# Block products of a ConvFFN: order of VectorE's work around the four pairs, and the rows of decayed sums in one buffer

## What is computed

```python
def conv_ffn(h, P, i):
    g = dwconv(h @ P['ffn_w_gate'][i], P['ffn_conv_w'][i])
    u = h @ P['ffn_w_up'][i]
    return (jax.nn.gelu(g) * u) @ P['ffn_w_down'][i]        # D_FF = 2816

# ssd_scan (layer 0), for each chunk of 128 tokens, direction and head
a_cs = jnp.cumsum(jnp.moveaxis(chunks(dt * a), -1, 1), axis=-1)
seg = a_cs[..., :, None] - a_cs[..., None, :]
decay = jnp.where(causal, jnp.exp(jnp.where(causal, seg, 0.0)), 0.0)
cb = jnp.einsum('bclhn,bcshn->bhcls', cm, bm) * decay
```

## Time and profile before

| | us |
|---|---|
| median of 3 runs | 1918.06 |
| lowest, highest | 1913.84, 1918.71 |
| the profiled execution | 1917.92 |
| its span | 1916.2 |

### The profile page before, as it was taken

How to read it: one execution, slowest core, us unless ns; L and a number is a source line. 1 busy time by engine, 2 the same in 40 slices (tenths; PEclk the granted TensorE clock), 3 DMA queues, 4 the chain that set the end, 5 groups by cost and what they waited for, 6 DMA issues and landing times.

```text
span 1916.2 us, 34733 instructions
## 1 busy us (share of the span) xinstructions
PE 1857.5 (97%) x13240; PEld 1775.7 (93%) x13240; DVE 1182.6 (62%) x2247; ACT 681.0 (36%) x1108; POOL 694.6 (36%) x389
## 2 busy tenths in 40 slices
PE   5999999999999999999999999999999999999997
PEld 3998888888999999999999999977899999999997
DVE  5767788776623777675554354567567676755543
ACT  4443332223313333333333321157433333333332
POOL 1232222223232336355335433433223363453352
PEclk9999999999999999999999999999999999999998
DMA  8335454554533212213212432211322232132221
GB/s 296 108 104 164 143 170 144 167 166 154 174 121 88 77 61 84 74 58 99 76 53 73 145 92 86 89 36 33 103 66 67 59 94 75 58 88 77 60 66 72
DMA packets 263965, 192.76 MB, mean 101 GB/s; under 512 B 25514, under 2 KB 247078, under 8 KB 263350
## 3 DMA queue, kind: packets, MB, share of 16 engines
q1 hardware_dynamic: 258694, 182.78, 31.2%
q10 hardware_dynamic: 5168, 8.58, 1.3%
HBM read 181.29 MB, written 10.04 MB: 100 GB/s over the span
## 4 chain that ended last, share of the span: by engine, by line
PE 86%; issue 5%; DVE 4%; ACT 2%; POOL 1%; DMA 1%; SPq 0%; POOLq 0%; ACTq 0%; DVEq 0%
PE ps L712 46%; PE ps L715 23%; PE ps L1044 5%; PE ps L782 2%; POOL w_lo L629 1%; PE ps L1190 1%; PE ps L974 1%; PE ps L1170 1%; PE ps L1136 1%; DVE x L2192 1%; DVE act_lo L1827 1%; DVE w_mix L2178 1%; ACT sp L1619 1%; PE ps L1209 0%; PE ps L959 0%
## 5 line engine op out<-in xcount | busy, mean ns | idle before, releaser
L629 POOL TENSOR_TENSOR w_lo<-raw,w_hi 128x1024 fp32r<-128x1024 f32 x212 | 532.0, 2513 | 1031.5 <-ACT w_hi L1243 1025.3
L712 PE MATMUL ps<-act_hi,w_hi 128*128 128x322 f32 x2752 | 640.5, 314 | 4.8 <-DVE act_lo L1827 2.2
L712 PE MATMUL ps<-act_lo,w_hi 128*128 128x322 f32 x2752 | 634.4, 312 | 0.0
L715 PE MATMUL ps<-act_hi,w_lo 128*128 128x322 f32 x2752 | 633.1, 311 | 0.0
L712 PEld LDWEIGHTS ps<-act_hi,w_hi 128*128 128x128 f32 x2752 | 462.4, 190 | 18.2 <-issue 14.9
L712 PEld LDWEIGHTS ps<-act_lo,w_hi 128*128 128x128 f32 x2752 | 464.2, 189 | 3.4 <-issue 3.4
L715 PEld LDWEIGHTS ps<-act_hi,w_lo 128*128 128x128 f32 x2752 | 467.0, 190 | 0.0
L1243 ACT ACTIVATE w_hi<-raw 128x1024 fp32r<-128x1024 f32 x212 | 222.7, 1052 | 250.1 <-PE ps L715 191.8
L1044 PE MATMUL ps<-quad_hi,w_hi 128*128 128x322 f32 x336 | 106.7, 318 | 8.4 <-DVE x L2192 8.4
L1911 DVE SCALAR_TENSOR_TENSOR ft<-fg,par,ft 128x642 f32<-128x642 f32 x44 | 110.6, 2514 | 3.5 <-DVE ft L1910 2.5
L2244 DVE TENSOR_TENSOR fg<-ps,spread 128x642 f32<-128x642 f32 x44 | 36.3, 826 | 115.1 <-PE ps L715 103.9
(11 more groups left out here) (326 smaller groups left out, 2533.3 us busy)
## 6 DMA issues: line engine op xcount, KB each, us to landing
ada<-in_ada_w SPq DMA_DIRECT2D x40, 1024.0 KB, 6.0
raw<-in_ssd_w_in SPq DMA_DIRECT2D x44, 512.0 KB, 3.9
raw<-in_ffn_w_gate SPq DMA_DIRECT2D x44, 512.0 KB, 3.8
raw<-in_ffn_w_up SPq DMA_DIRECT2D x44, 512.0 KB, 3.8
raw<-in_na_w_qkv SPq DMA_DIRECT2D x24, 512.0 KB, 3.7
raw<-in_ffn_w_down SPq DMA_DIRECT2D x32, 320.0 KB, 3.1
first<-in_ada_w SPq DMA_DIRECT2D x16, 512.0 KB, 11.1
raw<-in_mix_w_out SPq DMA_DIRECT2D x16, 512.0 KB, 4.1
```

What stands on the lines that cost most here:

```text
L629: g.tensor_tensor(w_lo[:, s], raw[:, s % RAW], w_hi[:, s], ALU.subtract).then_inc(S["low_split"], 1)
L712: t.matmul(half_out(2 * tset, h), hi, chunk_of(src, k0 + k, cols), start=start and src is src_hi, stop=False)
L715: mm = t.matmul(half_out(2 * tset, h), lo, chunk_of(src_hi, k0 + k, cols), start=False, stop=stop)
```

## The change

In the FFN, `product` is cut in two, `gate_part` and `up_part`. At the end of a part VectorE now does `gate_part(late, 0)`, the four weight sums of the second pair, the four `pair_added`, and only then `up_part(late, 0)` with what follows it. `pair_added` of the first pair makes no weight sums. A11 is no longer added to `x` by itself: `first_sbuf` is added to A12 in PSUM (one `tensor_tensor` of 322 columns) and the sum to `x`. `pair_taken` counts six for each pair, and ScalarE may overwrite `first_sbuf` only when the previous pair's A12 was taken. In the mixer, `sum_rows` is one buffer of 5 x 128 columns, the fifth block being the context chunk's sums; `rows_of` is one matmul of 512 columns, and the context rows are four fp32r matmuls of 128 columns.

```diff
-        sum_rows = [at("sum_rows0", N0 + 2 * ROW, [P, 2 * P], F32R),
-                    nc.alloc_sbuf_tensor_at("sum_rows1", [P, 2 * P], F32R, offset=tri_at + 2 * P * 4)]
+        sum_rows = mix("sum_rows", [P, NC * P], F32R)
...
-            for n in range(LC):
-                bank, off = 4 + 3 * (n // 2), P + n % 2 * P
+            for n in range(NC):
+                bank, off = (4 + 3 * (n // 2), P + n % 2 * P) if n < LC else (4, 3 * P)
                 t.transpose(ps[0:2 * HEADS, bank, off:off + P], sc[:, n, K_SUM, :], ident[:])
...
-                for b in range(2):
-                    mm = t.matmul(ps[:, 5, 2 * b * P:2 * b * P + 2 * P], lhs, sum_rows[b][:], start=True, stop=True)
-                mm.then_inc(S["rows_ready"], 1)
+                t.matmul(ps[:, 5, :], lhs, sum_rows[:, 0:LC * P], start=True, stop=True).then_inc(S["rows_ready"], 1)
...
-                        lhs = col[:, LC * KINDS + K_DA, r, h:h + 1].broadcast_to([P, P])
-                        mm = t.matmul(ps[:, 5, (2 * h + r) * P:(2 * h + r + 1) * P], lhs, tri[:, r, :], start=True, stop=True)
+                        lhs = pick[:, r, h:h + 1].broadcast_to([P, P])
+                        mm = t.matmul(ps[:, 5, (2 * h + r) * P:(2 * h + r + 1) * P], lhs, sum_rows[:, LC * P:NC * P], start=True, stop=True)
...
-                                          (A12, 2, 2), (S4, 3, 2), (A22, 6, 3)):
+                                          (A12, 2, 1), (S4, 3, 1), (A22, 6, 2)):
...
-                            act.wait_ge(S["pair_taken"], TAKEN0 + 7 * (pair - 1) + 2)
+                            act.wait_ge(S["pair_taken"], TAKEN0 + 6 * (pair - 1) + 4)
...
-                    for b in range(2):
-                        row = ps[0:2 * HEADS, 4 + 3 * b, P:3 * P]
-                        st.did(v.memset(sum_rows[b][:].bitcast(F32)[4 * HEADS:P, :], 0.0))
...
+                    st.did(v.memset(sum_rows[:].bitcast(F32)[4 * HEADS:P, :], 0.0))
+                    for bank, c0, c1, off in ((4, 0, 2 * P, P), (7, 2 * P, 4 * P, P), (4, 4 * P, 5 * P, 3 * P)):
...
-                more = q < PAIRS - 1
+                more = 0 < q < PAIRS - 1
...
+                used_product(S2)
                 dve.wait_ge(S["pair_copied"], pair + 1)
-                to_x(A11, 0, 0).then_inc(S["pair_taken"], 1)
-                used_product(S2)
                 tt(both_sbuf[:], ps[:, banks[S2], 0:SW], first_sbuf[:], ALU.add).then_inc(S["pair_taken"], 1)
...
                 used_product(A12)
+                summed = ps[:, banks[A12], 0:SW]
+                st.then_wait(tt(summed, summed, first_sbuf[:], ALU.add))
                 to_x(A12, 0, 0).then_inc(S["pair_taken"], 1)
...
-                    if i % SK == SK - 1:
-                        part, late = i // SK, i + 1
-                        ins = product(late, 0)
+                    if ends:
+                        late = i + 1
+                        gate_part(late, 0)
+                        for j in range(4):
+                            weight_sum(p0 + 1, j)
+                        for q in range(PAIRS):
+                            pair_added(lay, p0 + q, q)
+                        ins = up_part(late, 0)
                         if part < SPARTS - 1:
                             quad_sums(late, 0, ins)
+                            quad_lows(late, 0)
                         else:
                             ins.then_inc(S["ffn_up"], 1)
-                        for q in range(PAIRS):
-                            pair_added(lay, (lay * SPARTS + part) * PAIRS + q, q)
-                        (quad_lows if part < SPARTS - 1 else plain_low)(late, 0)
+                            plain_low(late, 0)
```

More of the change, by code:

```diff
@@ L255, in trunk @@
         sto = mix("sto", [P, 2, NS])
[L258 to L259 removed]
+        sum_rows = mix("sum_rows", [P, NC * P], F32R)
+        assert o[0] <= N0
         wdt = at("wdt", CT + 10240, [P, C, 32])
@@ L1034, in pair_down @@
                 for r, operand, taken in ((A11, 0, before[0]), (S2, 5, before[1]), (S1, 1, before[2]), (S3, 4, before[3]),
-                                          (A12, 2, 2), (S4, 3, 2), (A22, 6, 3)):
+                                          (A12, 2, 1), (S4, 3, 1), (A22, 6, 2)):
                     bank = banks[r]
                     pe.wait_ge(S["pair_low"], 7 * pair + r + 1)
-                    pe.wait_ge(S["pair_taken"], 7 * pair + taken + TAKEN0)
+                    pe.wait_ge(S["pair_taken"], 6 * pair + taken + TAKEN0)
                     if q == 0 and r == A11:
@@ L1981, in _ @@
                     group_taken(0)
-                    for b in range(2):
-                        row = ps[0:2 * HEADS, 4 + 3 * b, P:3 * P]
-                        st.did(v.memset(sum_rows[b][:].bitcast(F32)[4 * HEADS:P, :], 0.0))
-                        st.then_wait(v.tensor_copy(sum_rows[b][0:2 * HEADS, :], row))
-                        st.did(tt(sum_rows[b][2 * HEADS:4 * HEADS, :], row, sum_rows[b][0:2 * HEADS, :], ALU.subtract))
+                    st.did(v.memset(sum_rows[:].bitcast(F32)[4 * HEADS:P, :], 0.0))
+                    for bank, c0, c1, off in ((4, 0, 2 * P, P), (7, 2 * P, 4 * P, P), (4, 4 * P, 5 * P, 3 * P)):
+                        row = ps[0:2 * HEADS, bank, off:off + c1 - c0]
+                        st.then_wait(v.tensor_copy(sum_rows[0:2 * HEADS, c0:c1], row))
+                        st.did(tt(sum_rows[2 * HEADS:4 * HEADS, c0:c1], row, sum_rows[0:2 * HEADS, c0:c1], ALU.subtract))
                 for s in range(4):
@@ L2198, in taken @@
                 def taken(n):
-                    dve.wait_ge(S["pair_taken"], TAKEN0 + 7 * pair + n)
+                    dve.wait_ge(S["pair_taken"], TAKEN0 + 6 * pair + n)
+                used_product(S2)
                 dve.wait_ge(S["pair_copied"], pair + 1)
-                to_x(A11, 0, 0).then_inc(S["pair_taken"], 1)
-                used_product(S2)
                 tt(both_sbuf[:], ps[:, banks[S2], 0:SW], first_sbuf[:], ALU.add).then_inc(S["pair_taken"], 1)
@@ L2206, in pair_added @@
                     weight_sum(pair + 1, 0)
-                taken(2)
+                taken(1)
                 st.did(to_x(S2, 0, 1, sbuf=both_sbuf))
@@ L2228, in pair_added @@
                 used_product(A22)
-                taken(4)
+                taken(3)
                 to_x(A22, 1, 0).then_inc(S["pair_taken"], 1)
@@ L2238, in ffn, with gate_part @@
                 dve.wait_ge(S["rinv_ready"], (3, 5)[lay])
-                def product(i, k):
+                def gate_part(i, k):
                     n = f + k + 1 + 2 * i
@@ L2250, in product, with up_part @@
                     conv(par, w, w + 2 * FC, T, fg[k], ft[k]).then_inc(S["ffn_conv"], 1)
-                    if k == 1 and isinstance(i, int) and i < F_PLAIN // 2 and i % SK == SK - 1:
-                        for j in range(4):
-                            weight_sum((lay * SPARTS + i // SK) * PAIRS, j)
+                def up_part(i, k):
+                    n = f + k + 1 + 2 * i
                     used(b, i, 2 * k + 1)
@@ L2260, in product @@
                     return ins
+                def product(i, k):
+                    gate_part(i, k)
+                    return up_part(i, k)
                 def plain_low(i, k):
@@ L2287, in ffn @@
                 for i in range(F_PLAIN // 2):
+                    part, ends = i // SK, i % SK == SK - 1
+                    p0 = (lay * SPARTS + part) * PAIRS
                     for k in range(2):
                         if k > 0 or i == 0 or i % SK != 0:
-                            quad_sums(i, k, product(i, k))
-                            quad_lows(i, k)
-                    if i % SK == SK - 1:
-                        part, late = i // SK, i + 1
-                        ins = product(late, 0)
+                            gate_part(i, k)
+                            if ends and k == 1:
+                                for j in range(4):
+                                    weight_sum(p0, j)
+                            quad_sums(i, k, up_part(i, k))
+                            quad_lows(i, k)
+                    if ends:
+                        late = i + 1
+                        gate_part(late, 0)
+                        for j in range(4):
+                            weight_sum(p0 + 1, j)
+                        for q in range(PAIRS):
+                            pair_added(lay, p0 + q, q)
+                        ins = up_part(late, 0)
                         if part < SPARTS - 1:
                             quad_sums(late, 0, ins)
+                            quad_lows(late, 0)
                         else:
                             ins.then_inc(S["ffn_up"], 1)
-                        for q in range(PAIRS):
-                            pair_added(lay, (lay * SPARTS + part) * PAIRS + q, q)
-                        (quad_lows if part < SPARTS - 1 else plain_low)(late, 0)
+                            plain_low(late, 0)
                 i = F_PLAIN // 2
```

## The result

| | before | after |
|---|---|---|
| median us (4 runs each) | 1918.38 (1913.84 to 1918.71) | 1906.88 (1905.16 to 1907.59) |
| span of the profiled execution | 1916.2 | 1905.9 |
| TensorE idle in the block products, as traced | 8.4 | 5.6 |

The ratio is 0.9945, 95% interval 0.9933 to 0.9958: by the ratio 10.6 us less (8.1 to 12.9), faster by more than the 0.3% that can be told from no change; the medians are 11.5 apart. The forecast was 1906.8.

What follows compares the result with a forecast made beforehand. TensorE, 97% busy, bounds the kernel, so only removed instructions or its standstills count. Stalls -3.2, clock -4.6, mixer rows -3.6 and a transpose +0.2 sum to -11.2: 1906.8 us, range 1900 to 1915 for 8 in 10.

Steps and rivals of the forecast that it cites:

- Stalls: TensorE's four waits at the third pair's A11: 1.45 us lost in each group, 5.8 in place of 9.0, -3.2 us.
- The chain: VectorE's work in the second pair from both_sbuf to S4's add: 7.9 us, where TensorE comes after 6.47.
- The block of the fourth sum: Second pair: fourth weight sum collides with GpSimd's low part, ending at 744.09, not 743.62; without that 0.95 lost each.
- Clock: TensorE's 1.2 GHz stretches behind three of the four stalls: 2.4 GHz expected kept in all four, -4.6 us.
- Mixer: Context rows as short fp32r matmuls at weight-load price, 0.45 us less in eight steps, -3.6; one more transpose, +0.2.
- The late up work: up_part of the late tile after the fourth pair: costs nothing, covered with 1.9 us to spare before the next gate tile.
- VectorE's late start: Cause given for the stalls: VectorE begins the first pair late after up work, then makes next-pair sums in all but the last.
- rival A: TensorE never waits, if GpSimd's low parts, no longer bunched in the second pair, leave the sums free: -17, 1901; chance 0.12.
- B: Gain mostly paid back: stalls stay 2.0 us, most slow stretches stay, short matmuls cost as float32: 1912 to 1917; chance 0.27.
- C: Slower: third pair's VectorE chain slips beyond 1.2 us slack, so each group has two stalls: 1929; chance 0.05.
- D: FFN change does not reach TensorE, S4's event coming with another queue; only the mixer's -3.4 stays: 1914.5; chance 0.06.

Runs made afterwards that it cites:

- e6: Changed kernel with the fourth weight sum right behind the third, ahead of A12's two steps; same instructions, other order: 1903.99 us, 0.9931 of before.
- e2b: Changed kernel with up_part of the late tile again ahead of the four pairs, early weight sums kept: 1906.74 us, 0.9951 of before.
- e2: Changed kernel with the second pair's weight sums again made within the first pair, up_part still after the pairs: 1913.70 us, 0.9991 of before.
- e3: Changed kernel with A11 added to x by itself again and A12 not summed with first_sbuf: 1900.97 us, 0.9918 of before.
- e3b: Changed kernel with the fourth weight sum moved behind S4's add, nothing else: 1901.61 us, 0.9921 of before.
- e1: Changed kernel with its FFN half alone, the mixer's rows as before: 1909.05 us, 0.9966 of before.
- e5_both: Changed kernel with A11's own add back, no sum of A12 with first_sbuf, and the fourth weight sum behind S4's add: 1899.76 us, 0.9912 of before.

## Why the prediction was right, and where not

**Stalls, -3.2 forecast: -2.8 measured** (9.0 to 6.3). The chain was worked out as 7.9 us from `both_sbuf` to S4's add, TensorE went on after 8.03; the 0.1 missing is the first sum (0.54 from start to start in place of 0.46) and the time from the end of S4's add to the next matmul, taken as none. The block of the fourth sum, worked out from the earlier trace rows, came as 0.48 (0.94 in place of 0.46). The bound without that collision was 0.95 for each group; e6, where it is avoided by order, lost 1.10.

**Clock, -4.6 forecast: as measured** (seven slow stretches to four, 1.5 each). None of the four stalls has a slow stretch behind it, in any of the four traces with stalls of 1.56. That the sum came within 0.1 us of the median is partly luck: by the ratio the gain is 10.6, not 11.2, and a slow stretch more or less elsewhere moves a run by 1.5.

**Mixer, -3.4: -2.9 in this span** (10.3 - 2.8 - 4.6), -3.6 as the mean of the table's remainders (1896.7 against 1893.1). The fp32r matmul of 128 columns goes at the pace of its weight load, 0.11: four of them take 0.50 with the start of the next, 0.41 less than before in that step (0.45 forecast), 3.3 in eight. In the profiled execution some of it may have gone into a wait for `ada_w`, a transfer that was not among the steps of the prediction: L782 waits 2.0 us, before 1.1. In the nine traces with the short rows this wait is 1.0 to 2.1, in the three without 1.0 to 1.1. That the shorter steps cause the excess is not shown; the mixer-only trace, which has them, has 1.0.

**The late up work, costed at nothing: right** (e2b), and its cover is 2.43 us (1.9 forecast).

**Wrong in the main: why the stall was there.** The prediction put it to VectorE's late start (its second paragraph) and let the early sums only help this start. The late start made 0.6 us of the stall in the first part of each layer and nothing of it in the second; the blocked first sums and the add of `both_sbuf` made 1.5 in every group. e2b has a late start and short stalls, e2 an early start and the longest. What the early sums repaired in the main is the bunch of GpSimd's low parts. The sum came out right because its chain was taken from a pair of before whose low parts were not bunched; the bunch was named only as a hope of rival A. Rival A's time (1901) was reached with either of the two edits that shorten the chain (e3, e3b), not with the change.

**The other rivals.** B had the right parts (the block, the short matmul) with the wrong sizes. C's second stall never came: no trace has a gap at a fourth pair. The prediction left its third pair 1.2 us of slack; in the trace S4's add ends at 739.87 and the fourth pair's S1 begins at 741.00, 1.1 later. D is excluded by e1.

## What to carry to other kernels

Where two engines block each other, try another order before you remove work: 0.47 us for the blocked fourth sum came from order alone, and an add moved out of a wait into the chain cost 1.0 us although it made the program shorter. Measure a chain both where nothing is bunched and where it is, and ask which engine's queue is bunched and by whom; here moving the sums ahead paid mostly by what it let GpSimd do earlier. A stall on TensorE can have an echo in the clock, so the last 0.4 us that turn 1.95 lost into 1.56 can be worth 1.5 more. The kernel that came out, e5_both, takes 1899.8 us, 0.9912 of before (0.9894 to 0.9930), with some 0.25 us still lost in each group of block products.

## What was not expected of the hardware

After how many stalls the granted clock fell to 1.2 GHz, over all traces, by the time that the stall lost: 1.10, 1.29 and 1.56 us, none of 24 stalls; 1.95, two of 4; 2.56, four of 4; 2.71, three of 4. So from 1.95 to 2.71 us stalls of one length, in one kernel, may or may not cost the 1.5 us; what decides it stays open. That an fp32r matmul of 128 columns takes 0.11 us, half of a float32 one, was taken from a weight load and holds.

What stays open: why the wait for `ada_w` is anywhere between 1.0 and 2.1 us in the traces with the short rows; no run was made to take it away.
